# Differential attention and MLP block: projecting q, k and v twelve tiles ahead instead of sixteen, and splitting each head's weights in a small step instead of the largest

## What is computed

```python
u = rms_norm(x, norm1_g)
q, k, v = jnp.split(u @ w_in, 3, axis=-1)          # 8 heads; q and k have two maps of 64, v has 128 columns
q = rms_norm(q.reshape(B, S, H, 2, Dh), q_g); k = rms_norm(k.reshape(B, S, H, 2, Dh), k_g)
s = einsum('bqhmd,bshmd->bhmqs', q, k) * Dh ** -0.5  # chunk-causal mask, chunks of 64
p = softmax(s)
o = (p[:, :, 0] - lam * p[:, :, 1]) @ v
h = x + (rms_norm(o, sub_g) * (1 - lambda_init)) @ w_out
out = h + square(relu(rms_norm(h, norm2_g) @ mlp_w1)) @ mlp_w2
```

## Time and profile before

| what | value |
|---|---|
| median of 3 runs | 2808.23 us (2804.86 to 2811.44) |
| profiled execution, its own time | 2805.49 us |
| its span, first to last instruction | 2803.7 us |
| PE busy | 2721.1 us, 97% of the span |
| DVE, ACT, POOL busy | 68%, 54%, 38% |
| mean granted TensorE clock | 0.993 of full speed |

### The profile page before, as it was taken

The page is one execution under the profiler, slowest core; times in us unless marked ns, Lnnn a source line. Parts: engine busy times, 40 slices in busy tenths (PEclk is TensorE's granted clock), DMA queues, the critical chain, the costliest instruction groups (busy, mean ns, idle before and its releaser), DMA issues.

```text
span 2803.7 us, 42849 instructions
## 1 busy us (share of the span) xinstructions
PE 2721.1 (97%) x14784; PEld 2369.1 (84%) x14784; DVE 1896.4 (68%) x2726; ACT 1501.0 (54%) x2987; POOL 1076.4 (38%) x956
## 2 busy tenths in 40 slices
PE   7999999999999999979999999999999999999999
PEld 7898989989898999967887788888888888888887
DVE  6777787777778787775776666656555555666655
ACT  5666666666666666664554444444444444344443
POOL 5633424243433424331000354444343444444443
PEclk9999999999999999989999999999999999999999
DMA  8742424243242423223455996666667976666663
GB/s 267 263 142 86 161 97 153 94 150 113 94 153 86 161 97 128 98 86 142 155 183 188 353 371 239 236 235 251 269 247 277 364 280 237 233 232 239 235 236 130
DMA packets 181808, 544.09 MB, mean 194 GB/s; under 512 B 14736, under 2 KB 88208, under 8 KB 136592
## 3 DMA queue, kind: packets, MB, share of 16 engines
q1 hardware_dynamic: 180016, 541.25, 52.7%
q10 hardware_dynamic: 1632, 0.79, 0.1%
HBM read 470.81 MB, written 71.17 MB: 193 GB/s over the span
## 4 chain that ended last, share of the span: by engine, by line
PE 83%; issue 6%; DVE 4%; ACT 3%; DMA 2%; POOL 1%; SPq 0%; ACTq 0%; POOLq 0%; DVEq 0%
PE banks L2163 21%; PE banks L2139 21%; PE banks L421 17%; PE banks L666 5%; PE banks L563 4%; PE banks L565 4%; PE banks L638 4%; PE banks L825 3%; PE banks L668 2%; PE banks L513 2%; ACT pt_hi L647 1%; DMA u<-u_factors 1%; ACT p_all L605 1%; DVE mx L582 1%; DVE p_all L627 1%
## 5 line engine op out<-in xcount | busy, mean ns | idle before, releaser
L2139 PE MATMUL banks<-u,w 128*128 128x512 f32 x2688 | 614.6, 390 | 3.8 <-issue 2.0
L421 PE MATMUL banks<-w_hi,u_ring 128*128 128x384 f32 x2048 | 589.1, 347 | 10.8 <-DVE u_ring L1315 4.2
L2139 PEld LDWEIGHTS banks<-u,w 128*128 128x128 f32 x2688 | 505.5, 188 | 109.9 <-issue 3.8
L2163 PE MATMUL banks<-w,a_hi 128*128 128x512 f32 x1792 | 552.1, 389 | 1.5 <-issue 1.0
L1905 POOL TENSOR_TENSOR w<-w_raw,w 128x1024 fp32r<-128x1024 f32 x96 | 245.2, 2568 | 553.5 <-ACT w L1954 278.5
L605 ACT ACTIVATE p_all<-banks,bias 128x1024 f32<-128x1024 f32 (+7 forms) x384 | 331.7, 866 | 182.5 <-DVE bias L585 116.0
L2163 PEld LDWEIGHTS banks<-w,a_hi 128*128 128x128 f32 x1792 | 336.3, 188 | 72.3 <-issue 2.3
L421 PEld LDWEIGHTS banks<-w_hi,u_ring 128*128 128x128 f32 x2048 | 375.9, 188 | 15.6 <-issue 9.7
L2163 PE MATMUL banks<-w,a_lo 128*128 128x512 f32 x896 | 348.8, 389 | 0.0
L451 POOL TENSOR_TENSOR qk_rs<-qk_var,minus_half 128x4 f32<-128x4 f32 x128 | 129.4, 1011 | 563.4 <-DVE qk_var L445 563.4
L421 PE MATMUL banks<-w_lo,u_ring 128*128 128x384 f32 x1024 | 344.6, 337 | 0.0
(11 more groups left out here) (151 smaller groups left out, 4724.3 us busy)
## 6 DMA issues: line engine op xcount, KB each, us to landing
u<-u_factors SPq DMA_DIRECT2D x224, 1024.0 KB, 9.4
u_ring<-u_scratch SPq DMA_DIRECT2D x112, 1024.0 KB, 5.2
w_raw<-in_mlp_w SPq DMA_DIRECT2D x128, 512.0 KB, 6.7
u_scratch<-u_ring SPq DMA_DIRECT2D x16, 1024.0 KB, 5.0
u_factors<-q_hi SPq DMA_DIRECT2D x23, 512.0 KB, 4.4
u_factors<-q_lo SPq DMA_DIRECT2D x23, 512.0 KB, 4.3
w_raw<-in_a_w_in SPq DMA_DIRECT2D x90, 128.0 KB, 4.6
p_all<-in_x SPq DMA_DIRECT2D x16, 512.0 KB, 5.7
```

The lines of the kernel that those rows point to most:

```text
L421: last = pe.matmul(proj[:, 0:3 * HD], u[:, part, kt, :], w[:, kt, :], start=(kt == 0 and part == 0 and w is w_hi), stop=(kt == KT - 1 and ...
L2139: last = pe.matmul(banks[:, UP_BANKS[p] + f, :], w[:, 2 * k2 + k, f * P:(f + 1) * P], u[:, :, part, k, :], start=(STARTS[p] and k2 == 0 an ...
L2163: last = pe.matmul(banks[:, DOWN_BANKS[p] + t, :], a[:, p % 2, f, t * P:(t + 1) * P], b[:, f, :], start=(STARTS[p] and f == 0 and a is a_h ...
```

## The change

It does these things:

1. Projection runs twelve tiles ahead (`LEAD = 12`), so step a projects tile a + 12. The loop at the start has 12 iterations in place of 16; since all 16 tiles must still be normed and turned there, some iterations turn two tiles (`TURNED_WITH`). Steps j = 0 to 3 of the last head now project the last four tiles.
2. A head's weights now change behind tile n = 16 h + 15, which is projected in step j = 3 (`SPLIT_AT`), a small step. ACT, DVE and POOL split them there, and POOL has three of the four low parts, between its work for that step.
3. In `first_step` PE does the late values of tile a-2 between the two maps' scores, and the two pieces of the second half of the projection stand behind turnings of probabilities.
4. In the last head the high parts of `w_out` can be made only when a slot of `u_ring` has been projected for the last time, so each waits for its own slot; `high_w_out` and `low_w_out` move one step later (the last two pieces to step j = 4), and `pe_product` waits for each piece by itself.

The core of the diff:

```diff
+LEAD = 12
+SPLIT_AT = NT - LEAD - 1
+TURNED_WITH = ((1,), (2,), (3,), (4, 5), (6,), (7,), (8, 9), (10,), (11,), (12,), (13,), (14,), (15,))
...
     def high_w_out(act, kt):
-        if kt == 0:
-            act.wait_ge(proj_half, 2 * ALL)
+        act.wait_ge(proj_half, 2 * (ALL - US + kt // 2 + 1))
...
             for kt in range(part * HALF, part * HALF + HALF):
+                if t == 0 and d == 0:
+                    pe.wait_ge(w_out_lo_set, kt + 1)
...
# POOL
         def small_step(a, n):
...
+            splits = j == SPLIT_AT and h + 1 < H
+            if h == H - 1 and j == US:
+                low_w_out(pool, KT - 2)
+                low_w_out(pool, KT - 1)
+            if splits:
+                low_weights(pool, h + 1, 0)
             if n < ALL:
                 pool_factor_qk(pool, n)
                 pool_norm_qk(pool, n)
                 low_v(pool, n)
+            if splits:
+                low_weights(pool, h + 1, 2)
             if j:
                 pool_output(pool, a - 1)
-            if h == H - 1 and j <= 3:
-                low_w_out(pool, 2 * j)
-                low_w_out(pool, 2 * j + 1)
+            if splits:
+                low_weights(pool, h + 1, 3)
+            if h == H - 1 and 1 <= j < US:
+                low_w_out(pool, 2 * j - 2)
+                low_w_out(pool, 2 * j - 1)
...
# ACT
-        for j in range(NT):
-            if j + 2 < NT:
-                x_square(j + 2)
-            if j + 1 < NT:
-                high_u(j + 1)
+        for j in range(LEAD):
+            for t in TURNED_WITH[j]:
+                if t + 1 < NT:
+                    x_square(t + 1)
+                high_u(t)
...
+            if j == SPLIT_AT and h + 1 < H:
+                act_split_weights(act, h + 1, (0, 1))
             if a >= 2:
                 act_norm_output(act, a - 2)
...
                 act_square_output(act, a - 1)
+            if j == SPLIT_AT and h + 1 < H:
+                act_split_weights(act, h + 1, (2, 3))
...
# DVE, small_step
+            if j == SPLIT_AT and h + 1 < H:
+                low_weights(dve, h + 1, 1)
             if n < ALL:
                 dve_sum_qk(dve, n)
...
# PE
         def first_step(a, n, nb):
             pe_scores(pe, a, 0)
-            pe_scores(pe, a, 1)
             for g in late_values(a - 2):
                 pe_values(pe, a - 2, g)
+            pe_scores(pe, a, 1)
             if n < ALL:
                 pe_project(pe, n, 0)
             pe_turn_p(pe, a - 1, 0)
             pe_turn_p(pe, a - 1, 1)
+            if n < ALL:
+                pe_project(pe, n, 1, (0,))
             pe_values(pe, a - 1, 0)
             pe_turn_p(pe, a - 1, 2)
             pe_values(pe, a - 1, 1)
-            if n < ALL:
-                pe_project(pe, n, 1, (0,))
             pe_turn_p(pe, a - 1, 3)
-            pe_values(pe, a - 1, 2)
             if n < ALL:
                 pe_project(pe, n, 1, (1,))
+            pe_values(pe, a - 1, 2)
             pe_values(pe, a - 1, 3)
```

More of the change, by code:

```diff
@@ L1003, in sync @@
         store_u(NT - 2)
-        load_u(sp, NT)
         store_u(NT - 1)
-        for n in range(NT + 1, NT + 3):
-            load_u(sp, n)
         for a in range(ALL):
             h, j = split(a)
-            if a + NT + 3 < ALL:
-                load_u(sp, a + NT + 3)
-            if j == 4 and h + 2 < H:
+            if NT <= a + LEAD + 3 < ALL:
+                load_u(sp, a + LEAD + 3)
+            if j == SPLIT_AT + 3 and h + 2 < H:
                 load_weights(sp, h + 2, range(4))
@@ L1116, in big_step @@
                 pool_output(pool, a - 2)
-            if j == NT - 1 and h + 2 < H:
-                low_weights(pool, h + 2, 0)
-                low_weights(pool, h + 2, 1)
             if n < ALL:
@@ L1211, in small_step @@
                 act_turned_p(act, a - 1, g)
+            if h == H - 1 and j == US:
+                high_w_out(act, KT - 2)
+                high_w_out(act, KT - 1)
             if t >= 1:
                 act_turned_u2(act, t - 1)
+            if j == SPLIT_AT and h + 1 < H:
+                act_split_weights(act, h + 1, (0, 1))
             if a >= 2:
@@ L1248, in big_step @@
                 act_turned_u2(act, t - 1)
-            if j == NT - 1 and h + 2 < H:
-                act_split_weights(act, h + 2, (0, 1))
             act_turned_p(act, a - 1, 0)
@@ L1269, in big_step @@
                 act_sums_u2(act, t - 1)
-            if j == NT - 1 and h + 2 < H:
-                act_split_weights(act, h + 2, (2, 3))
             if t >= 0:
@@ L1277, in scalar @@
             if a % NT >= BIG:
-                big_step(a, a + NT, nb)
+                big_step(a, a + LEAD, nb)
             elif a and a % NT == 0:
-                first_step(a, a + NT, nb)
+                first_step(a, a + LEAD, nb)
             else:
-                small_step(a, a + NT, nb)
+                small_step(a, a + LEAD, nb)
         act_output_low(act, ALL - 2)
@@ L1377, in small_step @@
         def small_step(a, n, nb):
-            t = output_tile(*split(a))
+            h, j = split(a)
+            t = output_tile(h, j)
             dve_max(dve, a, 0, 0)
@@ L1475, in tensor @@
         turn_u(0)
-        for j in range(NT):
-            if j + 1 < NT:
-                turn_u(j + 1)
+        for j in range(LEAD):
+            for t in TURNED_WITH[j]:
+                turn_u(t)
             pe_project(pe, j, 0)
@@ L1511, in small_step @@
             t = output_tile(*split(a))
+            if a == 0:
+                pe_project(pe, n, 0)
+                pe_project(pe, n, 1)
             pe_scores(pe, a, 0)
@@ L1515, in small_step @@
                 pe_turn_p(pe, a - 1, 0)
-            if n < ALL:
+            if a and n < ALL:
                 pe_project(pe, n, 0)
```

51 lines of the change are left out of this document (20 added, 31 removed).

## The result

| what | before | after |
|---|---|---|
| median | 2807.97 us (5 runs) | 2850.78 us (2849.18 to 2851.55, 5 runs) |
| ratio to before | 1 | 1.0152 (95%: 1.0141 to 1.0164) |
| profiled execution, its own time | 2805.49 us | 2850.76 us |
| span | 2803.7 us | 2848.6 us |
| PE busy | 2721.1 us, 97% | 2736.8 us, 96% |

A forecast was written before the change was run, and what follows sets the result against it. PE, busy for 97% of the span, was taken as the bound. Terms -14.3 (A), -6.6 (B), +4.6 (E), +43.1 (C) and +7 (D) gave +33.8 on 2805.5; with 2.7 to the median, 2842 us, range 2816 to 2860.

The forecast's parts named there:

- C: Step 4 of seven heads: projection waits for low parts of the split weights, 6.16 us a head, +43 us.
- D: Slower PE clock behind those waits in step 4, 1 us for each of seven, +7 us, bounds 0 and +14.
- E: Last head, steps 0 to 4: -0.3 us in steps 0 to 3, +4.9 in step 4, together +4.6 us.
- A: Start, up to step 1's first projection: last tile turned sooner and waits gone, -14.3 us.
- B: first_step of six heads: part of the projection's second half fills a wait for DVE, -6.6 us.
- the two waits in step 4: Sign, heads 0 to 6: projection matmuls wait about 5 us for POOL's low part and about 1 for DVE's.
- the tile at 98: Sign, start: tile 15 is turned at about 98 us, instead of 100.55.
- the turning's 6 us in the last head: Sign, last head: a turning waits about 6 us for `ot_lo`.
- slices with a granted clock under 9: Sign: the profile's slices show granted clock under 9 at seven places one head apart.
- rival 2: Clock and last head worse: each 5 us wait brings a 1.2 GHz stretch losing 2 us; 2850 to 2866, chance 0.09.
- Rival 1: POOL's queue alone, no mutual blocking or clock drop: 4.0 us a head in step 4, 2820 us, chance 0.19.
- Rival 3: Faster: the split in step 4 is hidden, under 0.5 us a head, 2792 us, chance 0.09.

The follow-up runs named there:

- run 7: Changed kernel with 24 unused matmuls between the projection's halves in step 4 of seven heads, keeping PE busy in the wait: 2837.78 us, ratio 1.0103.
- Run 5: Changed kernel with POOL's three low parts ahead of the factor of q and k, and ACT's four high parts together: 2819.84 us, ratio 1.0044.
- run 4: Changed kernel with all four low parts of a head's weights on DVE, none on POOL, and ACT's four high parts together: 2807.49 us, ratio 0.9997.
- run 6: Changed kernel with low part 1 given from DVE to POOL, so that POOL makes all four: 2853.50 us, ratio 1.0160.
- Run 10: The version of run 9 with the last two pieces of w_out (6 and 7) split in step 3 of the last head as well: 2803.10 us, ratio 0.9981.
- run 9: Changed kernel with the changes of run 4 and run 8 together: 2805.48 us, ratio 0.9987.
- run 8: Changed kernel with the last head's w_out split moved: ACT's high parts behind its turned output, all low parts on DVE: 2850.87 us, ratio 1.0148.
- run 2: Kernel before the change with only PE's new order in first_step: 2829.08 us, ratio 1.0074.
- run 1: Changed kernel without the seven splits of weights, all heads projected with the first head's weights: 2792.39 us, ratio 0.9944.
- run 3: Changed kernel with PE's order in first_step put back as before: 2862.92 us, ratio 1.0193.

## Why the prediction was right, and where its numbers were off

**C was right in mechanism and size.** Forecast 43.1 us, measured 54.8 - 13.0 (the clock, run 7) = 41.8. The order of the queues gave the two losses, their places and their lengths (0.9 and 5.2 us forecast, 0.9 and 5.0 by the starts; PE's idle time is 0.7 and 4.8). Run 5 shows that the place in the queue makes more than half of C and D; runs 4 and 6 show that DVE and POOL shut each other out, which made the part on DVE nearly useless while POOL works. Of the two forms of the sum, with the lock and 10 us lower without it, the measured one is the first's: DVE's part ends at 462.06, where the forecast's chain, put on this trace's axis, has 462.3 with the lock and 460.8 without.

**D was mis-sized.** It was put at 7 us (1 a head, "a stretch at the lower level"), between 0 and 14; it is 13.0 (1.86 a head). A loss of 1 us is what six or seven matmuls of the projection lose at the lower level, half of the second half; but all of its twelve run at 0.32 us in place of 0.174, and 12 x 0.15 = 1.8. On the span the forecast is 11.1 us too low (33.8 against 44.9), and D is 6.0 of it, E 3.0, A 1.9 and the places put at nothing 2.0; C and B go the other way by 1.3 and 0.5. Between the medians the distance is only 8.8 us (2842 against 2850.8), because the 2.7 us added for the profiled execution of before were not there after: that nearness is luck.

**E had its sum near and its place wrong.** +4.6 was forecast and +7.6 measured. The step that failed: "In step 4 the turning of p(115) waits for `ot_lo` [...] 5.9 of wait against 1.05 now". It waits 0.61. PE stands in step 3 instead, 2.39 us for a slot of the turning banks behind a combination that took 2.85 us beside POOL, and 1.44 us in front. The chain to `ot_lo` itself was near the forecast's, 6.4 us against 7.4 (ACT takes the last values at 1300.91, the turning starts at 1307.29), but PE stood through its first part in step 3. The forecast's -0.3 for steps 0 to 3 was +3.3. And in step 4 it is the product that waits, 3.5 us for low parts 6 and 7, with the clock down behind it. That step 4 still came to +4.3, beside +4.9 forecast, is luck, and the value is uncertain: in the other runs that leave the last head's queues alone the step takes 23.4 to 25.7 us, +2.0 to +4.3. The change itself names it, a wait for each piece by itself and the last pieces in step 4; I had counted the pieces' durations on POOL and not the place of ACT's high parts behind the exponentials. Run 10 beside run 9 shows what this place costs: 3.5 us less in this step when the last pieces stand in step 3 (6.8 less than in the changed kernel, the moves of runs 4 and 8 included).

**A was 1.9 us too large.** Tile 15 is turned at 99.81, not 98: the pace of the tiles holds to the end, and half a projection less ahead of it made no difference that can be seen. In the nine other profiled executions with this start it is turned 0.1 to 3.1 us later still, so A may well be smaller than the -12.4 of this execution. The rest, one projection and two waits less, came as worked out (8.0 us from that turning to the projection of step 1, 7.9 forecast). **B** was right (-7.1 against -6.6), but not a gain by itself (run 2), which the forecast did not need and did not see.

**The signs.** Of those named ahead, the two waits in step 4 (one of them filed under "issue"), DVE's longer low part, the PE share of 96% and the wait of 1.31 us in step 0 came as said (0.3 of the last is left). Three did not: the tile at 98, the turning's 6 us in the last head, and slices with a granted clock under 9. The last could not have shown: a slice is 71 us long, and 4.5 us at half clock take 3% off it.

**The rivals.** The measured time lies at the lower end of rival 2's (2850 to 2866), whose mechanism was the clock and the last head: it is that rival's terms, D at its bound and E above its value, laid on the forecast's C; 0.09 was too small a chance for it. Rival 1, POOL's queue alone at 4.0 us a head, is excluded by the rows (6 us). Rival 3 is what run 1 makes of it, 2792 us, and only with the split left out.

**What stays open:** the +2.0 us outside the named places, of which 1 lies behind step 4 of the last head, and 3 us of run 3 together with its one long step; the start's length varies by 3 us from one execution to another, step 4 of the last head by 2.4, and I did not try to bring these apart.

## What to carry to other kernels

When work is moved to another step, write down for each engine the queue between the moved instruction and its consumer, with the durations of rows that exist: that gave the largest term here to about 3%. A wait and the slow stretch at the lower clock behind it have to be summed together, and the second can be read off by giving PE something useless to do in the wait. A reordering that fills a wait can depend on another part of the same change: tried alone, B turned from a gain of 7 us into a loss of 20.

## What the runs showed of the hardware

- DVE beside POOL, both reading two operands from SBUF: 2.31 us instead of 0.95 for the same 128x768 subtraction (run 4 and the changed kernel), 2.85 us instead of 0.75 for a combination of 128x512 beside a 128x1024 subtraction on POOL. Four low parts on DVE alone, 3.8 us, beat one on DVE and three on POOL, also where POOL's stand as early as they can (2807.5 us in run 4, 2819.8 in run 5).
- Behind a wait of 4.8 us all of the twelve matmuls that followed ran at 1.2 GHz (0.32 us apart, 0.174 at full clock), and the values behind them again at 2.4 GHz (granted clock 0.52 from 469.4 to 473.9, 1.00 behind). With PE busy in that wait there was none of it. Behind the wait of 3.79 us of run 2 the clock fell later: 1.00 for the first 1.2 us of matmuls, then 0.51 for 3.5 us.
